# Rolled row loops and one block of loads in the first output projection of a hybrid decoder block

## The reference

```python
h = jnp.concatenate([meta, x], axis=1)
...
mix = (gates[..., :D_MODEL] * y_a + gates[..., D_MODEL:] * y_b) @ w_out[l]
h = h + _rms_norm(mix, norm_mix_post[l])
hn = _rms_norm(h, norm_ffn_pre[l])
up = hn @ ffn_w_up[l]
a = _causal_dwconv(up[..., :D_FF], ffn_conv_w[l], ffn_conv_b[l])
f = (jax.nn.gelu(a, approximate=True) * up[..., D_FF:]) @ ffn_w_down[l]
h = h + _rms_norm(f, norm_ffn_post[l])
```

## Time and profile before

| what | value |
|---|---|
| median of 3 runs | 3455.92 us |
| lowest and highest | 3452.01 and 3461.46 us |
| the profiled execution | 3455.92 us, span 3454.1 us |
| matmuls on PE | busy 3201.9 us, 93% of the span |
| VectorE, ScalarE | busy 1787.8 us and 1216.3 us |
| granted TensorE clock, mean | 0.964 of full speed |
| moved by DMA | 409.23 MB, 118 GB/s over the span |

### The profile page before, as it was taken

One profiled execution on the slowest core, in us unless ns is written; L12 is line 12 of the kernel. 1 busy time (PEld: TensorE's weight loads), 2 busy tenths in 40 slices (PEclk: granted clock), 3 DMA queues, 4 the chain that ended last, 5 costly groups with the idle time before them and its releaser, 6 DMA issues. The chain is left out here.

```text
span 3454.1 us, 69468 instructions
## 1 busy us (share of the span) xinstructions
PE 3201.9 (93%) x26506; PEld 2843.6 (82%) x26506; DVE 1787.8 (52%) x3179; ACT 1216.3 (35%) x1971; POOL 121.3 (4%) x126
## 2 busy tenths in 40 slices
PE   6999999999875888878998989999999999899998
PEld 6999999999754677768997868999988888688887
DVE  6566652222276566655434458766686666311433
ACT  5211114433374344443113335444454444311211
POOL 0000000000000123220000000000000000000000
PEclk8999999999876999989999999999999999999999
DMA  5333333343466243334334742333332222411442
GB/s 157 96 104 127 118 138 117 127 130 123 156 240 196 68 95 91 93 92 138 130 107 157 219 156 74 112 113 103 121 123 79 90 80 69 152 50 42 147 122 86
DMA packets 350541, 409.23 MB, mean 118 GB/s; under 512 B 137152, under 2 KB 280384, under 8 KB 344304
## 3 DMA queue, kind: packets, MB, share of 16 engines
q1 hardware_dynamic: 350448, 407.99, 37.1%
HBM read 260.31 MB, written 147.59 MB: 118 GB/s over the span
## 5 line engine op out<-in xcount | busy, mean ns | idle before, releaser
L434 PE MATMUL psum<-x_hi,proj_w_hi 128*128 128x344 f32 x1632 | 533.8, 327 | 4.4 <-DVE proj_w_lo L521 4.4
L434 PE MATMUL psum<-x_lo,proj_w_hi 128*128 128x344 f32 x1632 | 524.0, 321 | 0.0
L434 PE MATMUL psum<-x_hi,proj_w_lo 128*128 128x344 f32 x1632 | 522.6, 320 | 0.0
L2547 PE MATMUL psum<-up_x,up_w_hi 128*128 128x512 f32 (+2 forms) x1540 | 353.3, 351 | 12.9 <-ACT up_w_hi L2568 6.9
L2553 PE MATMUL psum<-up_x,up_w_hi 128*128 128x512 f32 (+2 forms) x1540 | 353.7, 352 | 0.8 <-DVE up_x L2705 0.8
L2550 PE MATMUL psum<-up_x,up_w_lo 128*128 128x512 f32 (+2 forms) x1540 | 353.1, 351 | 0.0
L434 PEld LDWEIGHTS psum<-x_hi,proj_w_hi 128*128 128x128 f32 x1632 | 308.7, 189 | 5.8 <-issue 4.5
L434 PEld LDWEIGHTS psum<-x_lo,proj_w_hi 128*128 128x128 f32 x1632 | 308.5, 189 | 1.4
L434 PEld LDWEIGHTS psum<-x_hi,proj_w_lo 128*128 128x128 f32 x1632 | 308.3, 189 | 0.0
L2547 PEld LDWEIGHTS psum<-up_x,up_w_hi 128*128 128x128 f32 x1540 | 259.6, 190 | 54.8 <-issue 7.0
L2553 PEld LDWEIGHTS psum<-up_x,up_w_hi 128*128 128x128 f32 x1540 | 260.9, 191 | 42.6 <-DVE up_x L2705 1.1
(11 more groups left out here) (336 smaller groups left out, 5530.0 us busy)
## 6 DMA issues: line engine op xcount, KB each, us to landing
scratch_hidden<-up_hidden SPq DMA_DIRECT2D x44, 512.0 KB, 2.6
down_a_raw<-scratch_hidden SPq DMA_DIRECT2D x32, 704.0 KB, 6.3
up_weight<-in_w_up_sets SPq DMA_DIRECT2D x42, 512.0 KB, 4.5
up_weight<-in_w_up_sets SPq DMA_DIRECT2D x84, 256.0 KB, 3.3
proj_area<-scratch_s_tab SPq DMA_DIRECT2D x32, 608.5 KB, 3.8
scratch_s_tab<-proj_area SPq DMA_DIRECT2D x16, 1089.0 KB, 4.3
proj_weight<-in_w_in_tiles SPq DMA_DIRECT2D x34, 512.0 KB, 4.0
scratch_gates<-proj_mixed SPq DMA_DIRECT2D x16, 1032.0 KB, 4.0
```

The costliest lines, as they stand in the source:

```text
L434: mm = nc.tensor.matmul(psum[:, bank(v, n), 0:N_TOK], w[:, v, k, :], x[:, k, cols], start=(k == 0 and w is w_hi and x is x_hi), stop=(k == ...
L2547: nc.tensor.matmul(out, w_hi[:, q % 7, k, :], x_hi(step)[:, k, c0:c1], start=opens and k == 0, stop=False, skip_group_check=True)
```

## The change

Only SP's instructions in `token_projection` change. For mixout the written-out turns become: `row_tiles(1)` for r = 2 and 3, a loop on SP over i = 2 to 5 (r = 4 to 11), then a block outside any loop, then a loop over i = 6 and 7 (r = 12 to 15). The loop variable is a register, so addresses and wait values are computed on SP. `load_first` is gone; in the block all 16 loads from `h_normed` are issued one behind another, quarter by quarter, and behind them both weight loads. The block stands after `store_next(8)` of turn r = 11 and before `load_acts(12)` of turn r = 12. It first waits until the stores of the transposed tiles 0 to 7 have landed. `store_next` addresses `next_x` with a register and a rearranged pattern of the same 512 KB. The `else` branch issues the same transfers as before, through the shared `row_tiles`. Every transfer of before is still made, with the same size.

```diff
-
             def store_next(r, u):
                 sp.wait_ge(turned_out, r + (1 + SLOTS))
-                sp.dma_start(next_x[r], next_rows[:, u]).then_inc(next_stored[u], 16)
-
-            def load_first(r):
-                sp.wait_ge(next_stored[r % SLOTS], 16 * (r // SLOTS) + 32)
-                at = CONV_W - 1 + r * P % UP_COLS
-                for quarter, k in ((0, 0), (2, K4)) if r < UP_COLS // P else ((1, 0), (3, K4)):
-                    sp.dma_start(next_first[quarter][:, :, at:at + P], next_x[r, :, k:k + K4]).then_inc(next_loaded, 16)
-
-            def row_tile(r, u):
-                load_acts(part, r, P, r * P)
-                load_rows(r, u, P, r * P)
-                store(r - 2, u, P, (r - 2) * P)
+                sp.dma_start(next_x[bass.ds(r, 1)].rearrange("o p k t -> p (o k) t"), next_rows[:, u]).then_inc(next_stored[u], 16)
+
+            def row_tiles(i, first_next):
+                for u in range(SLOTS):
+                    r = 2 * i + u
+                    load_acts(part, r, P, r * P)
+                    load_rows(r, u, P, r * P)
+                    store(r - 2, u, P, (r - 2) * P)
+                    if next_norm and (first_next or u):
+                        store_next(r - 3, 1 - u)
 
             if next_norm:
                 for u in range(SLOTS):
                     sp.sem_inc(next_stored[u], 16)
-                ahead = list(next_loads)
-                for r in range(2, TILES):
-                    row_tile(r, r % SLOTS)
-                    if r >= 3:
-                        store_next(r - 3, (r - 3) % SLOTS)
-                    if 0 <= r - 5 < 2 * UP_COLS // P:
-                        load_first(r - 5)
-                    elif r >= 5 and ahead:
-                        buffer, source, sem = ahead.pop(0)
-                        sp.dma_start(buffer, source).then_inc(sem, 16)
+                READY = 6
+                row_tiles(1, False)
+                with sp.Fori(2, READY) as i:
+                    row_tiles(i, True)
+                for u in range(SLOTS):
+                    sp.wait_ge(next_stored[u], 16 * ((2 * UP_COLS // P) // 2) + 16)
+                for n, (quarter, k, at_t) in enumerate(((0, 0, 0), (1, 0, UP_COLS), (2, K4, 0), (3, K4, UP_COLS))):
+                    for r in range(UP_COLS // P):
+                        sp.dma_start(next_first[quarter][:, :, CONV_W - 1 + r * P:CONV_W - 1 + (r + 1) * P], next_x[at_t // P + r, :, k:k + K4]).then_inc(next_loaded, 16)
+                for buffer, source, sem in next_loads:
+                    sp.dma_start(buffer, source).then_inc(sem, 16)
+                with sp.Fori(READY, TILES // 2) as i:
+                    row_tiles(i, True)
             else:
                 with sp.Fori(1, TILES // 2) as i:
-                    for u in range(SLOTS):
-                        row_tile(2 * i + u, u)
+                    row_tiles(i, False)
```

## The result

| | before | changed |
|---|---|---|
| median of 6 runs | 3457.52 us | 3477.18 us |
| lowest to highest | 3452.01 to 3465.17 | 3474.91 to 3486.27 |
| span of the profiled execution | 3454.1 us | 3476.6 us |
| ratio | | 1.0052, 95% interval 1.0041 to 1.0064 |

The ratio puts the loss at 18 us, between 14 and 22. The forecast was 14.7 us. On the 3455.9 us that it started from, the ratio gives 3473.9 us, inside the range; the raw median of the six runs, 3477.2, lies 0.2 us above its upper end.

The account below looks back on a forecast made before the run. PE was taken to bound the kernel, with transfers hidden under it. A 12.5 us stall before tile 12 plus 2.2 us of clock gave 14.7 us, so 3455.9 + 14.7 = 3470.6 us, range 3459 to 3477.

Parts of the forecast that it names:

- PE sets the pace; thinner DMA gives nothing back: Mixout turns 5 to 14: PE never idles at 11.74 to 11.84 us per tile, so removing loads there is worth 0.
- The loops cost nothing: SP's turns as loops: register moves, compares and branches fit SP's idle time and load_acts' slack; cost nothing.
- Tile 12 lands 26.15 us after `store_next(8)`: Mixout, load_acts(12): 1.65 + 15.1 + 5.3 + 1.9 us of saturated DMA plus 2.2 us, landing at 2006.5.
- The slack of 11.8 us: Mixout: tile 12 may land by 1994.0 without cost, 11.8 us after its present issue.
- The stall of 12.5 us: Mixout, before tile 12's products: PE starts at 2009.0 in place of 1996.47, a stall of 12.5 us.
- The clock, 2.2 us: PE's restart at tile 12: clock fallen to 0.50, 11 matmuls at 0.2 us more each, 2.2 us.
- Nothing else is late: After tile 12: held-back rows, stores, load_acts(13), later tiles, meta tile and ffn_up's start all in time; no added loss.
- Rival 1: Block in mixout drains faster, all of it at 416 GB/s: time 3464.3 us; chance 0.14.
- Rival 2: Mixout: the burst does not delay tile 12, which lands by 1994.0; 3456 us, within noise; chance 0.09.
- The reason I gave: SP's queue in mixout is served in order, so load_acts(12) waits for all bytes ahead of it, 7.34 MB with its own.

Follow-up runs that it names:

- E2: Kernel before with SP's turns 5 to 12 as loops, pairs of loads kept in their turns, weights at turns 13 and 14; ratio 1.0001.
- E8: Changed kernel with its block of loads moved behind turn 15 and the second loop gone, timed against the kernel before; ratio 1.0003.
- E12: The kernel before against itself, as a control; ratio 1.0001, stretch 217.3 us.
- E5: The changed kernel again, no edit, timed against the kernel before; ratio 1.0046, stretch 230.5 us.
- E1: Kernel before with turns written out and only the block of 16 + 2 loads moved behind store_next(8); ratio 1.0031, stretch 230.2 us.
- E3: As E1, but the block holds only the 16 loads, weight loads at turns 13 and 14; against the kernel before, ratio 1.0025.
- E4: As E3, but tiles 0 to 3 keep their pairs in turns 5 to 8, leaving a block of 8 loads; ratio 0.9995 against before.
- E10: Kernel before with a block of 12 loads behind store_next(8), pairs for tiles 0 and 1 in turns 5 and 6, weights at 13 and 14; ratio 1.0016.
- E6: Block of 16 + 2 loads with turns written out, but load_acts(12) issued ahead of it; ratio 1.0034 against the kernel before.
- E7: As E1, but the 16 loads move 2048-byte rows, so the result differs from the reference's; ratio 1.0035 against the kernel before.
- E9: Kernel before with the 16 + 2 loads issued by GpSimd after tile 8 is turned out, not by SP; ratio 1.0023.
- E11: Kernel before with four of the loads in each of turns 12 to 15 and both weight loads after turn 15; ratio 1.0003.

## Why the prediction was right

- **PE sets the pace; thinner DMA gives nothing back.** Right. With the pairs gone from turns 5 to 12 the tiles still follow at 11.77 to 11.79 us.
- **The loops cost nothing.** Right for the loops alone: E2, and E8 with the change's own loops. For loops and block together see E12.
- **Tile 12 lands 26.15 us after `store_next(8)`.** ACT takes it up 26.6 us after (2013.84 - 1987.28), 25.6 in E5, 25.4 in E1. By parts of the sum: the 16 loads 14.5 us (4.19 MB at the 290 GB/s of E1) for my 15.1; the weights 4.9 us by the pauses of E1 and E3 for my 5.3; half a block 13.3 us in all for my 13.3. With these parts the sum is 25.1 us, 1 us under mine, and E5 and E1 lie nearer to it. Estimating a transfer from the difference of DMA share times duration between two whole tiles was 4% too high for the loads and 8% for the weights.
- **The slack of 11.8 us**, 13.6 after `store_next(8)`. Right: E4 just fits into it, E10 with four loads more overshoots by 3.3 us, and the runs with a pause give 13.8 to 14.0.
- **The stall of 12.5 us.** 12.7, 11.7 and 11.5 us in three profiles. That the first lies within 0.2 us of the forecast is luck in part: the sum priced the transfers 1 us too high, and that profile has the dip in the DMA share told under E5.
- **The clock, 2.2 us.** Taking 217.1 us as the stretch without a pause, what is left beside the pause is 2.5, 1.7, 1.6, 2.5, 2.6, 3.0, 2.4 and 1.7 us in the eight profiles with one (changed, E5, E1, E3, E6, E7, E9, E10), 2.3 in the mean. The starts of PE's matmuls show that this is the clock: against 0.23 us from one to the next, the first twenty intervals after the pause take 2.5, 1.7, 1.7, 2.3, 2.5, 2.9, 2.0 and 1.7 us more. The size is right. What I wrote before E10, that PE idles too briefly there for its clock to fall, was wrong.
- **Nothing else is late.** Right: from tile 2 to tile 15 PE waits once.
- **Rival 1, a faster drain,** fails: 290 GB/s, far nearer to 277 than to 416. The Trainium skill's 3 cycles per packet ("DMA: Bandwidth & Descriptors", Why small descriptors are slow), 366 GB/s by my estimate from them, was 26% too high here. (By my own sum that estimate gives a stall of 8.9 us and 3467.0 in all, not 8.5 and 3466.5; nothing else hangs on it.)
- **Rival 2, no loss,** is what E4, E8 and E11 show for a smaller, a later and a spread block. Its deciding point, landing by 13.6 us, was the right one.
- **The reason I gave was incomplete.** I put the loss on the queue's order, and in rival 2 no loss on tile 12 overtaking. E6 and E9 show that letting tile 12 overtake leaves a pause of 6.9 and 5.6 us, about half of E1's 11.5 or more, and moves it to tile 13.

The total by the ratio, 18 us, is 3 us over the forecast. The stretch accounts for 13.4 to 15.4 of it; the rest is within the interval of the ratio (from 14 us) and not explained.

None of the versions is faster than the kernel before: PE has no idle time in this stage that a change of SP's order could remove. E8 and E11 equal it, and E8 does so with the loops of the change.

## What to carry to other kernels

Before transfers are gathered into a burst, work out two numbers from the trace of the kernel as it is: how long after the burst's place the next load on the critical path may land, and how many us of saturated DMA the burst and everything ahead of that load take. If the second is smaller, the burst is free, however long it holds up the issuing engine; if larger, the difference is the pause, plus some 2 us for TensorE's clock (1.6 to 3.0 here). Moving the one load ahead of the burst, or the burst to another queue, passed on 5.6 to 6.9 us of the pause to the next load here; spreading the burst by the spare DMA time of each turn, or putting it behind the last critical load, pays it.

## What the runs showed of the hardware that I had not expected

- TensorE's clock can fall after the engine has resumed: in E10 PE paused for 3.33 us, ran 0.9 us at full clock, then 3.4 us at half. In the changed kernel it fell within a 12.7 us pause and stayed low for 5.0 us after.
- A burst issued by GpSimd did not yield to SP's loads (E9): `load_acts(13)` shared the engines with it and took 18.0 us to land, where the loads of that kind take 5.0 in the median of the same run.
- Loads with 2048-byte rows began at 284 GB/s and reached 384 only some 6 us into the burst (E7); the 512-byte ones ran at a flat 290 (E1).
